# Three sums of squares as two passes of rounded halves in a two-layer hybrid trunk

## What is computed

```
q = rms_norm(a_q.reshape(bsz, L, FOX_HEADS, FOX_HEAD_DIM), fox_q_gain[l])
k = rms_norm(a_k.reshape(bsz, L, FOX_HEADS, FOX_HEAD_DIM), fox_k_gain[l])
...
o_b = hgrn2(...)
o_b = rms_norm(o_b, hgrn_o_gain[l].reshape(HGRN_HEADS, HGRN_VAL_DIM))
...
mix = jnp.concatenate([o_a, o_b, o_c], axis=-1)
x = x + mix @ w_out[l]
```

## Time and profile before

| | |
|---|---|
| median of 3 runs (lowest, highest) | 1032.58 us (1032.25, 1032.63) |
| the profiled execution's own time | 1033.05 us |
| its span in the profile | 1031.3 us |
| TensorE busy / weight loads | 99% / 98% |
| VectorE, ScalarE, GpSimd busy | 66%, 51%, 20% |
| granted TensorE clock | 1.0 of full speed |

### The profile page before, as it was taken

The page is one execution under the profiler, slowest core; times in us unless marked ns, Lnnn a source line. Parts: engine busy times, 40 slices in busy tenths (PEclk is TensorE's granted clock), DMA queues, the critical chain, the costliest instruction groups (busy, mean ns, idle before and its releaser), DMA issues.

```text
span 1031.3 us, 22763 instructions
## 1 busy us (share of the span) xinstructions
PE 1023.4 (99%) x9714; PEld 1006.2 (98%) x9714; DVE 680.3 (66%) x850; ACT 523.5 (51%) x628; POOL 205.0 (20%) x291
## 2 busy tenths in 40 slices
PE   8999999999999999999999999999999999999998
PEld 7999999999899999999999999999998999999998
DVE  7666656788668555555566665668987667555554
ACT  5645434565587534343475454436456765434341
POOL 0000899800002000000020019996000020000000
PEclk9999999999999999999999999999999999999999
DMA  8746454434325464545555555453442265464541
GB/s 301 269 158 209 164 200 162 162 128 161 124 83 204 164 209 164 202 164 200 176 205 207 181 186 204 163 204 123 153 138 92 92 228 204 164 203 163 203 163 42
DMA packets 26821, 178.44 MB, mean 173 GB/s; under 512 B 3121, under 2 KB 4161, under 8 KB 5761
## 3 DMA queue, kind: packets, MB, share of 16 engines
q1 hardware_dynamic: 25632, 173.03, 47.8%
q10 hardware_dynamic: 1008, 4.05, 1.1%
q0 software_dynamic: 112, 0.40, 0.1%
HBM read 176.42 MB, written 1.05 MB: 172 GB/s over the span
## 4 chain that ended last, share of the span: by engine, by line
PE 96%; DVE 2%; DMA 1%; SPq 0%; ACT 0%; issue 0%; DVEq 0%; ACTq 0%
PE ps L815 30%; PE ps L816 30%; PE ps L817 30%; DMA raw<-stream 1%; PE ps L968 1%; PE ps L1021 1%; PE ps L1086 1%; DVE lo L1228 0%; DVE in_lo L1427 0%; PE ps L1082 0%; SPq L363 0%; PE ps L1043 0%; ACT hi L577 0%; PE ps L1062 0%; PE ps L1031 0%; PE ps L1149 0%
## 5 line engine op out<-in xcount | busy, mean ns | idle before, releaser
L1228 DVE TENSOR_TENSOR lo<-raw,hi 128x2048 fp32r<-128x2048 f32 x130 | 302.7, 2337 | 200.0 <-ACT hi L577 199.9
L815 PE MATMUL ps<-xg_hi,hi 128*128 128x256 f32 x1408 | 399.3, 284 | 2.3 <-DVE lo L1311 1.4
L816 PE MATMUL ps<-xg_lo,hi 128*128 128x256 f32 x1408 | 398.4, 283 | 0.0
L817 PE MATMUL ps<-xg_hi,lo 128*128 128x256 f32 x1408 | 398.4, 283 | 0.0
L577 ACT ACTIVATE hi<-raw 128x2048 fp32r<-128x2048 f32 x130 | 247.1, 1909 | 176.4 <-PE ps L817 170.8
L815 PEld LDWEIGHTS ps<-xg_hi,hi 128*128 128x128 f32 x1408 | 270.3, 192 | 2.9 <-issue 2.8
L816 PEld LDWEIGHTS ps<-xg_lo,hi 128*128 128x128 f32 x1408 | 270.3, 192 | 0.1
L817 PEld LDWEIGHTS ps<-xg_hi,lo 128*128 128x128 f32 x1408 | 270.3, 192 | 0.0
L815 PE MATMUL ps<-act_hi,hi 128*128 128x256 f32 x704 | 199.4, 283 | 0.6 <-DVE act_lo L1266 0.6
L816 PE MATMUL ps<-act_lo,hi 128*128 128x256 f32 x704 | 199.2, 283 | 0.0
L817 PE MATMUL ps<-act_hi,lo 128*128 128x256 f32 x704 | 199.2, 283 | 0.0
(11 more groups left out here) (317 smaller groups left out, 1339.0 us busy)
## 6 DMA issues: line engine op xcount, KB each, us to landing
raw<-stream SPq DMA_DIRECT2D x160, 1024.0 KB, 4.9
par<-params ACTq DMA_DIRECT2D x2, 1463.0 KB, 9.1
raw<-stream SPq DMA_DIRECT2D x8, 256.0 KB, 7.3
rows<-stream SPq DMA_DIRECT2D x2, 1024.0 KB, 6.9
x<-xT ACTq DMA_DIRECT2D x4, 256.0 KB, 6.6
out<-x SPq DMA_DIRECT2D x8, 128.0 KB, 2.0
con<-consts POOLq DMA_DIRECT2D x1, 371.5 KB, 6.6
mask<-masks POOLq DMA_DIRECT2D x1, 20.0 KB, 6.7
```

Of the source, the lines that this page charges most:

```text
L815: pe.matmul(acc, w_hi, a_hi, start=start, stop=False, skip_group_check=True)
L816: pe.matmul(acc, w_hi, a_lo, start=False, stop=False, skip_group_check=True)
L817: return pe.matmul(acc, w_lo, a_hi, start=False, stop=stop, skip_group_check=True)
L1228: v.tensor_tensor(lo[slot][:, :], raw[slot][:, :], hi[slot][:, :].bitcast(F32), ALU.subtract).then_inc(lo_written, 1)
```

## The change

The native fp32 matmuls of `fox_sums` and `hgrn_sums` become two fp32r matmuls each, on a rounded half and the rest, accumulated in the same bank. The 0/1 matrices are copied once to fp32r by ScalarE (layer 0, first in `functions`, in step 3 of the first network). For the queries and keys ScalarE's Square writes the rounded half directly; POOL, behind the clearing of `attn`, computes the plain square and subtracts. For the HGRN output VectorE copies the square to the rounded half and subtracts, behind `fox_probabilities(0)` and ahead of `split_in(4)`. `hgrn_sums` moves from k = 3 to k = 5 of `project(11)`. The new tiles lie over memory that is free at that time, except `sum_rows`, which is new (1 KB per partition).

```diff
+        sum_rows = sb("sum_rows", [P, 2 * P], F32R)
...
+        fsq_lo = orms_r[:, 0, :].rearrange("p (w c) -> p w c", w=2)
+        osq_lo, osq_hi = orms_r[:, 0, :], orms_r[:, 1, :]
+        fsq_all = orms[:, 1, :, :].rearrange("p h t -> p (h t)").rearrange("p (w c) -> p w c", w=2)
...
-        halves = con[:, 2 * P:3 * P]
+        ones_r, halves_r = sum_rows[:, 0:P], sum_rows[:, P:2 * P]
...
                 sum_squares(l * 3 + 1)
                 pool.memset(attn[:, :, :], 0.0).then_inc(attn_cleared, 1)
+                for w in range(2):
+                    t = fqk[:, w, :, :].rearrange("p a t -> p (a t)")
+                    pool.wait_ge(proj_dve, l * 9 + 6 + w)
+                    pool.tensor_tensor(fsq_all[:, w, :], t, t, ALU.mult).then_inc(fsq_plain, 1)
+                    pool.wait_ge(fsq_plain, l * 2 + w + 1)
+                    pool.wait_ge(fsq_ready, l * 2 + w + 1)
+                    pool.tensor_tensor(fsq_lo[:, w, :], fsq_all[:, w, :], fsq_hi[:, w, :].bitcast(F32), ALU.subtract
+                                       ).then_inc(fsq_lo_ready, 1)
                 sum_squares(l * 3 + 2)
...
                 def functions():
 
+                    if l == 0:
+                        e.activation(sum_rows[:, :], con[:, P:3 * P], ACT.Copy).then_inc(rows_rounded, 1)
...
-                    e.activation(fsq[:, w, :], fqk[:, w, :, :].rearrange("p a t -> p (a t)"), ACT.Square
+                    e.activation(fsq_hi[:, w, :], fqk[:, w, :, :].rearrange("p a t -> p (a t)"), ACT.Square
                                  ).then_inc(fsq_ready, 1)
...
-                    pe.matmul(bank(6 + w), halves, fsq[:, w, :], start=True, stop=True).then_inc(fsum_done, 1)
+                    pe.wait_ge(rows_rounded, 1)
+                    pe.wait_ge(fsq_lo_ready, l * 2 + w + 1)
+                    pe.matmul(bank(6 + w), halves_r, fsq_hi[:, w, :], start=True, stop=False)
+                    pe.matmul(bank(6 + w), halves_r, fsq_lo[:, w, :], start=False, stop=True
+                              ).then_inc(fsum_done, 1)
...
-                    pe.wait_ge(osq_ready, l + 1)
+                    pe.wait_ge(osq_lo_ready, l + 1)
                     for b in range(2):
-                        last = pe.matmul(bank(2 + b), ones, osq[:, b * 512:(b + 1) * 512], start=True, stop=True)
+                        c = slice(b * 512, (b + 1) * 512)
+                        pe.matmul(bank(2 + b), ones_r, osq_hi[:, c], start=True, stop=False)
+                        last = pe.matmul(bank(2 + b), ones_r, osq_lo[:, c], start=False, stop=True)
...
-                project(11, {2: lambda: fox_transposes(0), 3: hgrn_sums, 6: fox_output})
+                project(11, {2: lambda: fox_transposes(0), 5: hgrn_sums, 6: fox_output})
...
                 fox_probabilities(0)
+                v.wait_ge(osq_ready, l + 1)
+                v.tensor_copy(osq_hi, osq[:, :]).then_inc(osq_hi_ready, 1)
+                v.wait_ge(osq_hi_ready, l + 1)
+                v.tensor_tensor(osq_lo, osq[:, :], osq_hi.bitcast(F32), ALU.subtract).then_inc(osq_lo_ready, 1)
                 split_in(4)
```

More of the change, by code:

```diff
@@ L180, in build @@
         span = [bf] + [sb(f"span{size}", [P, HEADS, T // size]) for size in LEVELS[1:]]
+        with ExitStack() as rounded:
+            orms_r = sb("orms_r", [P, 2, HEADS * T], F32R, rounded)
         orms = sb("orms", [P, 2, HEADS, T])
@@ L194, in build @@
         fv = sb("fv", [P, 2, 256], F32, fox_mem)
+        with ExitStack() as rounded:
+            fsq_hi = sb("fsq_hi", [P, 2, 2 * T], F32R, rounded)
         fsq = sb("fsq", [P, 2, 2 * T], F32, fox_mem)
@@ L320, in build @@
         fsum_done = sem("fsum_done")
+        fsq_plain = sem("fsq_plain")
+        fsq_lo_ready = sem("fsq_lo_ready")
+        rows_rounded = sem("rows_rounded")
+        osq_hi_ready = sem("osq_hi_ready")
+        osq_lo_ready = sem("osq_lo_ready")
         frn_ready = sem("frn_ready")
```

## The result

The changed kernel takes 1035.24 us, the median of 10 runs (1033.67 to 1036.33), against 1032.68 us (1032.25 to 1033.03) for the kernel before: ratio 1.0024, 95% interval 1.0016 to 1.0033. It is slower by 2.6 us, where 0.6 us had been forecast, and lies outside the range given (1029.3 to 1034.6 us). The profiled execution took 1035.08 us, 2.03 us more than that of the kernel before.

A forecast was written before the change was run, and what follows sets the result against it. TensorE, busy 99% of the span, was taken as the bound. The profiled 1033.05 us less 3.2 (sums) plus 3.8 (key wait) gave 1033.65, or 1033.2 us against the median of 1032.58; 8-in-10 range 1029.3 to 1034.6 us.

The forecast's parts named there:

- The gain on TensorE: Fox and HGRN sums: two fp32r passes replace each native matmul, 1.6 us less for each part, 3.2 us in all.
- the warm-up row: TensorE warm-up: 13 fp32r passes of 512 columns in 3.0 us, 0.23 us each, taken as the new passes' cost.
- What POOL takes from VectorE: Lo halves behind `take(6)`: POOL's square costs VectorE 0.83 us, the difference 1.08, 1.91 us per layer.
- Where it lands: Queries: hidden in VectorE's idle time; keys: all 1.91 us reaches TensorE's wait before `level(3)`, 3.8 us over two layers.
- The HGRN norm: `project(11)`: VectorE's copy and difference are ready before TensorE's sums at k = 5, hidden by 0.25 to 0.8 us.
- the one-input row: VectorE's L1542 in the earlier profile: at its pace the HGRN copy of 128x1024 would take 0.69 us.
- POOL holding VectorE up longer: Keys' operations: two of 1.48 us, all felt, 2.96 us per layer, 5.9 us in all, 1035.3 us; chance 0.12.

The follow-up runs named there:

- the first run with the sums at k = 3: The changed kernel with the HGRN sums left at k = 3 of `project(11)` instead of k = 5: 1038.00 us; 1036.48 us on another occasion.
- The changed kernel's second trace: The changed kernel unaltered, timed again on another occasion as yardstick: 1035.38 us, ratio 1.0026 to the kernel before.

## Why the prediction was wrong, point by point

- **The gain on TensorE.** Forecast 3.2 us, measured 3.16 in the trace. Right; the warm-up row was a good stand-in for the new passes.
- **What POOL takes from VectorE.** Forecast 0.83 us for the square and 1.08 for the difference, measured 0.85 and 1.09; the square alone, 0.84. Right, and the extension from 256 to 512 columns by the slope of the earlier trace rows held for what VectorE loses; POOL's own undisturbed length at 512 columns was not measured. By the Trainium skill's rule ("SBUF — State Buffer", section "Who interferes with whom") the other engine is blocked for the whole instruction; the trace agrees that they exclude each other, but what VectorE loses is about 0.2 us less than POOL's own length (0.74 us at 256 columns; 1.03 and 1.28 at 512 by the prediction's estimate), so 1.93 us in the lo halves and 1.91 at TensorE, and not 2.31.
- **Where it lands.** Right: the wait for the key went from 0.24 us late to 2.15, in both layers, and nothing gave it back. The fast version with POOL held back shows that it was the place and not the work.
- **The HGRN norm.** Right. The copy took 0.69 us, the pace of the one-input row, and TensorE did not wait at k = 5: in layer 0 VectorE's difference ended at 301.18 us, the sums began at 301.96. The cost of k = 3 was forecast as 0.6 to 1.2 us per layer; it is 0.54, a little below.
- **The step that failed** is the sentence on what follows the wait: "What TensorE does later hangs on itself and not on a clock of someone else, so nothing gives it back." It priced the standstill at its own length ("Two layers: 3.8 us more") and put what comes after it at nothing, without a reason from a row. The runs showed a second term: after 2.0 to 2.1 us without work TensorE's own clock fell to half for some 3.4 us, in none, one or both layers of an execution, 1.40 us in the profiled one and 1.3 to 1.5 in the others. With three idle VectorE products and no POOL work it comes too, with two it does not. With the measured terms and no fall the median would be 1032.68 less 3.16 plus 3.82, 1033.3 us; the median lies 1.9 us above it, and that is the whole error but 0.1 us. One fall explains 1.4 of the 1.9; the executions at the median have clock 0.998, one fall, and where the other 0.5 us comes from no trace shows. The profile before showed clock 1.0 everywhere, also in the warm-up stretch, and I took it as a constant. It was one only as long as no wait was long.
- **The rivals.** Slower was given 0.14, for POOL holding VectorE up longer. The time fell on that side, and even close to the 1035.3 us of that rival, but by chance: its 2.96 us per layer were not there, 1.91 were.

The Trainium skill has a rule on the clock ("TensorE: Matmul & The Clock Gate", "What's actually happening"): the clock is gated by how busy the engine has lately been, and idleness brings it back to the lower level. By that rule, the trace agrees that there are just two levels, 0.50 and 1.00 of full speed, and that the fall follows a standstill; had the prediction weighed it, it would have been a rival with the time of a fall per layer, up to 1036 us (1033.2 plus 2 times the measured 1.40).

## What to carry to other kernels

Where an engine moves work to POOL, look at what VectorE does at that very moment: a POOL `tensor_tensor` with SBUF inputs cost a VectorE instruction with two SBUF inputs almost its own length (0.545 us of 0.74 at 256 columns), and this is free only where VectorE idles anyway. Holding the POOL work back by one semaphore, to a stretch with slack, turned a loss of 2.6 us into a gain of 2.8. And a new wait of TensorE must be priced with its length and with what the clock does after it: shown here is no loss of clock at 1.4 us and up to 1.5 us per wait at 2.0 to 2.1 us. A list of runs that suddenly spreads is the cheapest sign.

## What the runs showed of the hardware that was not expected

- The clock fall comes at no fixed distance from the wait: in the changed kernel about 1.6 us after TensorE had resumed (264.14 against 262.56 us), in the kernel with three idle products 0.1 us after it (0.98 in the stretch 260 to 262, 0.58 in the next), and in layer 0 of the first run with the sums at k = 3 0.2 us before it (262.32 against 262.50 us). And it does not come every time: the same wait of 2.09 us in layer 1 passed without it. One more thing can be read in the traces with a fall in both layers: the two falls begin 512.0 us apart in all three, though the waits lie 511.1, 511.8 and 511.7 us apart. The changed kernel's second trace has the same mean clock in the two stretches in which it falls:

```profile
262.00:263.00 1.00, 1.00 (x66) 0.81 0.99 418
...
774.00:775.00 1.00, 1.00 (x10) 0.81 0.87 369
```

  So the moment of the fall is not set by the wait alone. What else sets it, and what decides whether it comes at all, is open; it was not tried.
- POOL does not always get its turn after one VectorE instruction. Behind `take(5)` its square was issued 0.16 us after the first of four lo halves, just as behind `take(6)`, but was held off through all four, and cost VectorE the time only in `extend(1)`:

```profile
247.79 2.49 DVE L1456 TENSOR_TENSOR in_lo<-raw,in_hi 128x512 fp32r<-128x512 f32 x4
...
250.53 1.50 DVE L1521 TENSOR_TENSOR qd<-qd,bf 128x512 f32<-128x512 f32 x1
251.95 1.75 DVE L1522 TENSOR_TENSOR key<-key,bf 128x512 f32<-128x512 f32 x1
...
247.95 3.53 POOL L566 TENSOR_TENSOR orms<-fqk 128x512 f32<-128x512 f32 x1 [41.29 <-DVE fqk L1479]
```

In this layer the price is nearly the same (0.82 and 1.07 us over 0.68; in layer 1 it is 0.62 and 1.07), only the place differs. The cause wasn't looked for, as VectorE idles behind it (1.30 us are left of the 3.21 of the earlier trace rows).
